# Group ends of a Mamba stage, a second block's first norms, and a first MLP unit, in another order

## What is computed

```python
xBC = jax.nn.silu(causal_depthwise_conv(xBC, conv_w, conv_b))   # 4 taps per channel
...
y = y * lax.rsqrt(jnp.mean(y * y, axis=-1, keepdims=True) + EPS)  # per group of 512
return y.astype(h.dtype) @ w_out
...
return rms_norm(h, g_final)                                     # end of the first block
...
hx = modulate(rms_norm_2(x, norm1), sh1, sc1)                   # start of the second block
ak, av, gk, gv, lrf, lrb, aq, gq, go, ga, gg = jnp.split(hx @ w_in, IN_OFFSETS, axis=-1)
...
x = x + gt2[..., None, :] * sq_relu_mlp(modulate(rms_norm_2(x, norm2), sh2, sc2), w_mlp1, w_mlp2)
```

## Time and profile before

| | |
|---|---|
| median of three runs | 1875.54 us (1874.74 to 1878.44) |
| the profiled execution's own time | 1872.59 us |
| its span, first to last instruction | 1870.8 us |
| TensorE busy in it | 1763.6 us (94%) |
| VectorE, ScalarE, GpSimd busy | 1009.3, 785.4, 716.7 us (54%, 42%, 38%) |
| mean granted TensorE clock | 0.976 of 2.4 GHz |

### The profile page before, as it was taken

How to read it: one execution, slowest core, us unless ns; L and a number is a source line. 1 busy time by engine, 2 the same in 40 slices (tenths; PEclk the granted TensorE clock), 3 DMA queues, 4 the chain that set the end, 5 groups by cost and what they waited for, 6 DMA issues and landing times.

```text
span 1870.8 us, 24943 instructions
## 1 busy us (share of the span) xinstructions
PE 1763.6 (94%) x8893; PEld 1406.8 (75%) x8893; DVE 1009.3 (54%) x1563; ACT 785.4 (42%) x1340; POOL 716.7 (38%) x795
## 2 busy tenths in 40 slices
PE   7998998988999999899999999999999989999998
PEld 5776776766777656678778888888878768888887
DVE  5978685477545784346658837656621442222122
ACT  4444353446446664335552245554432342223231
POOL 3644444532444013321113432223234545555553
PEclk9999999989999999999999999999999989999999
DMA  6332332211223001120108721121123323333332
GB/s 196 91 115 89 112 91 68 68 63 39 68 82 96 12 23 45 49 56 24 35 23 283 235 67 35 35 57 46 46 78 91 89 69 99 93 101 90 101 93 99
DMA packets 238793, 152.04 MB, mean 81 GB/s; under 512 B 7997, under 2 KB 223046, under 8 KB 238694
## 3 DMA queue, kind: packets, MB, share of 16 engines
q1 hardware_dynamic: 225894, 125.54, 23.4%
q10 hardware_dynamic: 12800, 25.17, 4.0%
HBM read 148.59 MB, written 2.10 MB: 81 GB/s over the span
## 4 chain that ended last, share of the span: by engine, by line
PE 75%; DVE 13%; ACT 6%; issue 4%; DMA 1%; SPq 1%; POOL 0%; DVEq 0%; ACTq 0%; POOLq 0%
PE ps L648 19%; PE ps L652 19%; PE ps L649 19%; DVE xs L1295 2%; PE ps L2062 2%; PE ps L2044 1%; PE ps L1545 1%; PE ps L1577 1%; PE ps L2051 1%; PE ps L2505 1%; DMA ada_late<-w_ada 1%; DVE mod_late L2363 1%; DVE queries L1814 1%; PE ps L2045 1%; ACT wh L611 1%
## 5 line engine op out<-in xcount | busy, mean ns | idle before, releaser
L598 POOL TENSOR_TENSOR wl<-raw,wh 128x256 fp32r<-128x256 f32 (+1 forms) x775 | 693.3, 924 | 1091.7 <-ACT wh L611 1091.6
L648 PE MATMUL ps<-ah,wh 128*128 128x512 f32 (+1 forms) x1208 | 492.1, 407 | 18.2 <-DVE al L760 9.2
L652 PE MATMUL ps<-ah,wl 128*128 128x512 f32 (+1 forms) x1208 | 475.2, 393 | 0.1
L649 PE MATMUL ps<-al,wh 128*128 128x512 f32 (+1 forms) x1208 | 475.0, 393 | 0.0
L611 ACT ACTIVATE wh<-raw 128x1024 fp32r<-128x1024 f32 (+1 forms) x220 | 230.8, 1049 | 343.6 <-PE ps L652 329.9
L648 PEld LDWEIGHTS ps<-ah,wh 128*128 128x128 f32 (+1 forms) x1208 | 228.1, 189 | 83.0 <-issue 22.9
L652 PEld LDWEIGHTS ps<-ah,wl 128*128 128x128 f32 (+1 forms) x1208 | 227.9, 189 | 52.7 <-POOL wl L598 1.4
L649 PEld LDWEIGHTS ps<-al,wh 128*128 128x128 f32 (+1 forms) x1208 | 228.6, 189 | 47.4 <-issue 1.7
L648 PE MATMUL ps<-bh,wh 128*128 128x512 f32 (+1 forms) x588 | 236.4, 402 | 19.0 <-DVE resid L1410 13.1
L652 PE MATMUL ps<-bh,wl 128*128 128x512 f32 (+1 forms) x588 | 233.2, 397 | 0.9 <-POOL wl L598 0.8
L649 PE MATMUL ps<-bl,wh 128*128 128x512 f32 (+1 forms) x588 | 232.6, 396 | 0.0
(11 more groups left out here) (409 smaller groups left out, 2575.0 us busy)
## 6 DMA issues: line engine op xcount, KB each, us to landing
raw<-w_mlp SPq DMA_DIRECT2D x64, 512.0 KB, 3.8
raw<-w_in SPq DMA_DIRECT2D x52, 512.0 KB, 3.7
raw<-ssm_w_in SPq DMA_DIRECT2D x40, 512.0 KB, 3.7
ada_late<-w_ada ACTq DMA_DIRECT2D x16, 1024.0 KB, 6.7
ada_raw<-w_ada ACTq DMA_DIRECT2D x16, 512.0 KB, 4.3
raw<-ssm_w_out SPq DMA_DIRECT2D x16, 512.0 KB, 3.4
raw<-mla_w_in SPq DMA_DIRECT2D x11, 512.0 KB, 3.8
raw<-mla_w_out SPq DMA_DIRECT2D x8, 512.0 KB, 3.4
```

The costliest lines, as they stand in the source:

```text
L598: nc.gpsimd.tensor_tensor(wl[:, s, part], raw[:, s, part], wh[:, s, part].bitcast(F32), ALU.subtract).then_inc(lo_ready, LOW_PIECES * (par ...
L648: nc.tensor.matmul(dst, w_hi[k], x_hi[k], start=k == 0, stop=False)
L649: nc.tensor.matmul(dst, w_hi[k], x_lo[k], start=False, stop=False)
L652: ins = nc.tensor.matmul(dst, w_lo[k], x_hi[k], start=False, stop=k == n - 1)
```

## The change

Three places change, and no arithmetic does.

**Group ends.** The newest tap and the bias of each convolution move from VectorE to ScalarE (`newest_tap`, an Identity activation with a scale and a bias per channel) in the three groups that follow the first. Piece 4's is made from PSUM in `take_conv`, piece 5's after the heads, pieces 0 to 3 between the roundings of the norm (`high`). VectorE adds the two halves of the first output unit after its second and its third convolution of x instead of after all. In g = 2 the second output unit moves ahead of `turn_x`.

```diff
@@ -1001,10 +1001,10 @@
                 for n in range(8, 10):
                     projection("ssm", g, n)
                 output("ssm", g, g, 10, 5, 0)
+                output("ssm", g, g, 10, 5, 1)
+                turn_x(g + 1)
                 if g < GROUPS - 2:
-                    output("ssm", g, g, 10, 5, 1)
-                turn_x(g + 1)
-                output("ssm", g, g, 10, 5, 2 if g < GROUPS - 2 else 1)
+                    output("ssm", g, g, 10, 5, 2)
                 turn_b(g + 1)
                 if g < GROUPS - 2:
                     output("ssm", g, g, 10, 5, 3)
@@ -1013,6 +1013,8 @@
             for w in range(4):
                 output("ssm_last", 0, GROUPS - 1, 0, 0, w)
+        conv_column = lambda g, n: g * 4 + n if n < 4 else 16 + 4 * (n - 4) + g
...
@@ -1031,11 +1033,21 @@
         def act_mamba(act):
+            def newest_tap(g, n, src):
+                k = V_CONV + conv_column(g, n)
+                o = xs[:, n] if n < 4 else (bt, ct)[n - 4][:]
+                nc.scalar.activation(o, src, ACT.Identity, scale=V(k + PAD * CCH), bias=V(k + TAPS * CCH))
+            def newest_of(g, n):
+                newest_tap(g, n, conv_in[:, n, PAD:PAD + T])
             def take_conv(stage, i, g, n):
                 if n == 0 and g:
                     act.wait_ge(sem("conv_ready"), g * 6 + AHEAD)
                 act.wait_ge(unit_done, unit(stage, i, n) + 1 + CREDIT)
+                if g and n == 4:
+                    newest_tap(g, n, bank(n % 2))
                 nc.scalar.activation(conv_in[:, n, PAD:PAD + T], bank(n % 2), ACT.Copy).then_inc(acc_free[n % 2], 1)
                 split_ahead(act, stage, i, n)
@@ -1130,6 +1142,9 @@
...
+                act.wait_ge(acc_free[1], g * 9 + ACC0["ssm"][1] + 4)
+                act.wait_ge(sem("mix_ready"), g * GH + GH)
+                newest_of(g + 1, 5)
                 for p in range(4):
                     square(g, p)
                 scale(g)
@@ -1137,7 +1152,12 @@
                 nc.scalar.activation(zs[:, 0], zs[:, 0], ACT.Silu)
                 gate("ssm", g, g + 1, 1)
                 split_ahead(act, "ssm", g, 7)
-                for p in range(4):
+                high(g, 0)
+                for p in range(1, 4):
+                    newest_of(g + 1, p - 1)
+                    if p == 3:
+                        act.wait_ge(sem("gv_ready"), g * 4 + 4)
+                        newest_of(g + 1, 3)
                     high(g, p)
...
@@ -1286,12 +1306,14 @@
             def convolve(stage, i, g, n):
-                tap = lambda k: V(V_CONV + k * CCH + (g * 4 + n if n < 4 else 16 + 4 * (n - 4) + g))
+                tap = lambda k: V(V_CONV + k * CCH + conv_column(g, n))
                 o = xs[:, n] if n < 4 else (bt, ct)[n - 4][:]
                 dve.wait_ge(acc_free[n % 2], i * 9 + (1 + ACC0[stage][n % 2] + n // 2 + 1))
-                st(nc.vector.tensor_scalar(o, conv_in[:, n, PAD:PAD + T], tap(PAD), tap(TAPS), ALU.mult, ALU.add))
+                if g == 0:
+                    st(nc.vector.tensor_scalar(o, conv_in[:, n, PAD:PAD + T], tap(PAD), tap(TAPS), ALU.mult, ALU.add))
                 for k in range(PAD):
-                    st.wait()
+                    if g == 0 or k:
+                        st.wait()
                     ins_ = nc.vector.scalar_tensor_tensor(o, conv_in[:, n, k:k + T], tap(k), o, ALU.mult, ALU.add)
                     if k + 1 < PAD:
                         st(ins_)
...
@@ -1402,9 +1424,9 @@
-            def output(stage, i, n0, w):
+            def output(stage, i, n0, w, halves=(0, 1)):
-                for c in range(2):
+                for c in halves:
@@ -1433,15 +1455,18 @@
                 convolve("ssm", g, g + 1, 4)
                 convolve("ssm", g, g + 1, 5)
                 normed(g)
-                for n in range(4):
-                    convolve("ssm", g, g + 1, n)
+                convolve("ssm", g, g + 1, 0)
+                convolve("ssm", g, g + 1, 1)
+                output("ssm", g, 10, 0, (0,))
+                convolve("ssm", g, g + 1, 2)
+                output("ssm", g, 10, 0, (1,))
+                convolve("ssm", g, g + 1, 3)
                 if g < CTX_BLOCKS // 2:
                     take_modulation(g)
-                output("ssm", g, 10, 0)
+                output("ssm", g, 10, 1)
+                weigh_x(g + 1)
                 if g < GROUPS - 2:
-                    output("ssm", g, 10, 1)
-                weigh_x(g + 1)
-                output("ssm", g, 10, 2 if g < GROUPS - 2 else 1)
+                    output("ssm", g, 10, 2)
                 take_b(g + 1)
                 if g < GROUPS - 2:
                     output("ssm", g, 10, 3)
@@ -1883,12 +1908,12 @@
-        GAINED_BANK = 7
+        GAINED_BANK, FINAL_BANK = 7, 4
         def act_between(act):
             norm_act(act, "norm1", None, D, b=GAINED_BANK, eps=EPS * EPS)
             norm_high(act, "norm1", chunk(ah), lambda j: mod[:, j, 0:1])
-            norm_act(act, "final", None, D, dst=norm_sq[:, 1])
+            norm_act(act, "final", None, D, b=FINAL_BANK, dst=norm_sq[:, 1])
         def dve_between(dve):
@@ -1984,6 +2009,8 @@
                 main, side = K_BANKS[n]
                 if n == 0:
                     pe.wait_ge(acc_free[1], ACC0["gqa"][1] + 1)
+                else:
+                    pe.wait_ge(norm_rstd, 2 * NORM_AT["final"][0] + 1)
                 low = unit_high(pe, "gqa", 0, K_UNIT + n)
                 project(bank(main), "gqa", K_UNIT + n, chunk(ah), chunk(al), DC, P, low=low).then_inc(sem("k_projected"), 1)
                 project_ctx("gqa", K_UNIT + n, bank(side)[:, 0:CTX], P).then_inc(unit_done, 1)
@@ -1995,31 +2022,32 @@
                 nc.tensor.matmul(bank(6), ones[:], k_sq[n][:, 0:T], start=True, stop=True)
                 nc.tensor.matmul(bank(7)[:, 0:CTX], ones[:], k_sq[n][:, T:TA], start=True, stop=True).then_inc(sem("k_sums"), 1)
-            def project_v(half, tiles):
+            lows = {}
+            def project_v(half, tiles, ks=range(V_KS)):
                 s = slot("gqa", half)
-                unit_ready(pe, "gqa", 0, half)
+                if ks[0] == 0:
+                    lows[half] = unit_high(pe, "gqa", 0, half)
                 vh, vl = flat(wh, s, FULL, V_KS), flat(wl, s, FULL, V_KS)
-                for t in tiles:
-                    dst = bank((6, 7, 3)[t // 2])[:, t % 2 * CTX:(t % 2 + 1) * CTX]
-                    hi, lo, tok = (ah, al, t) if t < TT else (ch, cl, t - TT)
-                    tok = slice(tok * P, (tok + 1) * P)
-                    for k in range(V_KS):
-                        c = half * V_KS + k
+                for k in ks:
+                    lows[half](k, KVH * HD)
+                    for t in tiles:
+                        dst = bank((6, 7, 3)[t // 2])[:, t % 2 * CTX:(t % 2 + 1) * CTX]
+                        hi, lo, tok = (ah, al, t) if t < TT else (ch, cl, t - TT)
+                        tok, c = slice(tok * P, (tok + 1) * P), half * V_KS + k
                         nc.tensor.matmul(dst, hi[:, c, tok], vh[:, k], start=half == 0 and k == 0 and t % 2 == 0, stop=False)
                         nc.tensor.matmul(dst, hi[:, c, tok], vl[:, k], start=False, stop=False)
                         ins_ = nc.tensor.matmul(dst, lo[:, c, tok], vh[:, k], start=False, stop=c == DC - 1 and t % 2 == 1)
-                    if half and t in (1, 3):
-                        ins_.then_inc(sem("gv_projected"), 1)
+                        if half and k == V_KS - 1 and t in (1, 3):
+                            ins_.then_inc(sem("gv_projected"), 1)
                 return ins_
-            lows = {}
...
@@ -2064,13 +2092,18 @@
             pe.wait_ge(acc_free[1], ACC0["lr"][1] + 1)
             project_ctx("lr", 0, bank(1, slice(0, 32), slice(0, CTX)), 32).then_inc(sem("lr_ctx"), 1)
+            norm_pe_summed(pe, "norm1", norm_v[:, 2], GAINED_BANK)
+            norm_pe_summed(pe, "final", norm_v[:, 1], FINAL_BANK)
             project_v(0, range(TT, KT))
-            norm_pe_summed(pe, "norm1", norm_v[:, 2], GAINED_BANK)
-            norm_pe_summed(pe, "final", norm_v[:, 1])
             pe.wait_ge(acc_free[0], ACC0["lr"][0] + 1)
-            project(bank(0, slice(0, 32)), "lr", 0, chunk(ah), chunk(al), DC, 32, before=norm_chunk(pe, "norm1")).then_inc(unit_done, 1)
-            pe.wait_ge(norm_rstd, 2 * NORM_AT["final"][0] + 1)
-            project_v(0, range(TT)).then_inc(unit_done, 1)
+            ready = norm_chunk(pe, "norm1")
+            for k in range(DC):
+                lr_done = project(bank(0, slice(0, 32)), "lr", 0, chunk(ah), chunk(al), DC, 32, before=ready, ks=[k])
+                if k == DC - 1:
+                    lr_done.then_inc(unit_done, 1)
+                if k % 2:
+                    v_done = project_v(0, range(TT), [k // 2])
+            v_done.then_inc(unit_done, 1)
             project_v(1, range(KT)).then_inc(unit_done, 1)
             project_q(0, range(DC))
             project_k(0)
```

(23 more changed lines are left out.)

4 lines of the change are left out of this document (2 added, 2 removed).

## The result

The changed kernel takes 1850.53 us (median of four runs, 1849.85 to 1852.46). The kernel before, run beside it, had 1875.14 (four runs, 1867.33 to 1878.44): ratio 0.9876, 95% interval 0.9845 to 0.9908. In a larger set, 19 runs of the kernel before have a median of 1870.26 (1866.27 to 1879.26) and four more of the changed one 1851.91: ratio 0.9893, 0.9865 to 0.9920. So the gain is 18.4 us by the larger set and 24.6 by the smaller, and the kernel before scatters by 13 us from run to run, the changed one by 3.

What follows compares the result with a forecast made beforehand. TensorE, busy 94% of the span, was taken as the bound, with waits and half clock to save: 8.4 + 7.4 + 5.5 + 5.8 + 1.3 = 28.4 us off 1872.6 gives 1844.2, plus 2.9 is 1847; range 1841 to 1856, some 83%.

Steps and rivals of the forecast that it cites:

- First two group ends: Norm's end to transposes in g = 0 and 1: removing TensorE's waits and half clock gains 8.4 and 7.4 us.
- ScalarE's later split: First output unit's split arrives some 0.6 us later; in g = 0 and 1 TensorE does modulation sums first, no loss.
- Third group end: Group end g = 2, first output unit to the heads: 18.3 us becomes 12.2, gain 5.5 after 0.6 for late split.
- the new wait before the state: Group end g = 2: no unit lies between transposes and state any more, so some 0.9 us of waiting stays open.
- Second block: Start of the second block: earlier sums and alternating lr and value matmuls gain 5.8 us, bounds 3.5 and 6.8.
- the wait before value unit 1: Second block: ScalarE may split for unit 1 only after lr is done, so TensorE waits 1.0 us.
- MLP: First MLP units: alternation gains 1.3 us, bounds 0 and 2, with half clock taken for 4.8 us at the start.
- Rival (c): Low clock comes elsewhere, as later gaps move: up to 4 us either way, 1843 to 1852; 71% together with the forecast.
- Rival (a): Second block and MLP: stretches alternate as written but at 1.2 GHz throughout; gain 10.4 us, time 1865; 4%.
- (b): Group ends: VectorE late at the transposes by 2.3 us or less, clock falls; 3 to 11 us back, middle 1853; 19%.
- (d): Group ends: ScalarE becomes the bound, splitting the first output unit late; whole turns negative at 9.5 us each, 1879; 2%.
- (e): Stalls only change places: as (b), and value and MLP splits return the second block's gains; under 4 us left, 1873; 4%.

Runs made afterwards that it cites:

- Experiment 8: Changed kernel with the modulation's one-column matmuls of the first two groups spread between the chunks of the two following projections: median 1849.27 us, ratio to before 0.9886.
- `both`: Changed kernel with spread modulation matmuls, and the first output unit's gate and split moved ahead in all three groups: 1843.71 us, ratio to before 0.9862.

## Why the prediction was nearly right

The forecast was 1847 us with 1841 to 1856, the result 1850.5: inside, on the slow side. Part of that is luck. The forecast's start, 2.9 us above the profiled execution, was the median of three executions, 1875.54; 19 runs of the same kernel have 1870.26. From there the same terms give 1842, and the gain of 28.5 us stands against 18.4 measured with the larger set and 24.6 with the smaller. Point by point:

**First two group ends,** 8.4 and 7.4 forecast, 7.4 and 5.9 measured. By the clock of the two traces VectorE's chain seems to match: first half added at 175.74 (forecast 175.7), second at 179.30 (179.4), last silu done 182.20 (182.4), transposes 183.03 (183.0). That is luck: the norm's sum stands at 155.15 before and 154.18 after. Counted from it, the steps come 1.0, 0.9 and 0.8 us later than forecast, and the transposes 28.85 us behind it instead of 27.85. The order of the steps was right. VectorE's rows for the two halves, and ScalarE's for the silu:

```profile
175.05 0.69 DVE L1432 TENSOR_TENSOR resid<-resid,ps 128x512 f32<-128x512 f32 x1 [1.19 <-PE ps L652]
...
178.62 0.68 DVE L1432 TENSOR_TENSOR resid<-resid,ps 128x512 f32<-128x512 f32 x1
```

```profile
181.57 0.63 ACT L1083 ACTIVATE xs<-xs 128x512 f32<-128x512 f32 x1 [2.20 <-DVE xs L1317]
```

The step that failed is the one that took ScalarE's later split as hidden by the modulation sums ("TensorE first has the modulation sums to do and does not notice"), a cost of nothing in the sum. Experiment 8 and `both` show what stands in its place: without any low clock the transposes still come at 28.84 and 28.85 us, 1.0 and 0.9 later than the sum had them, and with the split moved ahead as well at 26.94 and 26.96. The low clock behind the sums, which the first trace of before did not show in group 0, was missed too: in group 0 its 3.4 us cost nothing beside this chain, in group 1 its 6.8 us cost 0.6.

**Third group end,** 5.5 forecast, 6.0 measured in a trace without a low stretch there, 5.3 in the trace of the group ends alone, with one; against the other three traces of the old code, 5.0. The late split cost 0.7 us (forecast 0.6), the new wait before the state 0.63 (0.9).

**Second block,** 5.8 forecast, 5.5 measured, split 3.4 and 2.1 where the text had 3.5 and 2.3; the wait before value unit 1 is 1.09 (forecast 1.0).

**MLP,** 1.3 forecast, 0.3 to 0.9 at equal low clock: mis-sized. The wait before unit 2 is 0.28 us in the trace (0.5 to 1 forecast). The low stretch ended 2.8 us behind the start there, where 4.8 was forecast.

**Rival (c) was sized too small:** "up to 4 us either way", with a middle of zero. Outside the changed places the stages lost 4.5 us in this pair of traces, the larger part of the 5.7 that the profiled execution lies above the forecast's 1844.2. Between the two traces of the kernel before, the rest of the second block moved by +3.1 us, the rest of the first by +2.3 and the heads by -1.1. Rival (a), half clock throughout, is refuted: the second block's stage has no low clock in any of the nine traces with the alternation, and the MLP's runs at full clock once the low stretch that stood there already is over (19 matmuls in 4 us):

```profile
1490.00:1494.00 4.00, 4.00 (x19) 3.26 (x18) 4.00 (x7) 2.17 (x3) 0.00 (x0) 1.00 0.01 4
```

The Trainium skill, page "TensorE: Matmul & The Clock Gate", section "A second HAM failure mode: psum-queue depth-cycling", tells of another kernel whose clock swung while it cycled through PSUM banks; in this trace no swing follows from the alternation. (b) did not come: the silus end 0.8 to 0.9 us ahead of the transposes in all three groups. (d) was closer than its 2%: ScalarE did become a bound of the group ends, and its sign, TensorE waiting for `wh` at an output unit, stands in the third group with 2.50 us (1.85 before); but it is far from the 9.5 us a group that would have turned the gain. The sign of being right that failed is the clock of 1.00 at the first two group ends. (e) is refuted by the stage table.

**Left open:** what decides which gaps bring the low clock in an execution, and whether the changed kernel's smaller scatter (3 us in 8 runs against 13) comes from having fewer gaps. The group ends alone scatter by 8 us in four runs.

## What to carry to other kernels

Judge a change of a few us by the length of the changed stage between two fixed instructions, read at equal low-clock time, and not by the kernel's total: here a real gain of 5.5 us was invisible in the median of ten runs, and a step worth 2.1 us looked like a loss. Where only totals are at hand, set each run's time beside its own granted clock first: that took the scatter here from 13 us to a deviation of 0.9. When a stall on one engine goes, look for a distance that stays the same to 0.02 us in every group and every variant: it names the chain that bounds next, even where no wait is shown. Moving work to a second engine pays only if nothing that the first one waits for stands behind it there.

## What was not expected of the hardware

The clock can fall without any wait of TensorE. Behind 32 one-column matmuls (row at 155.04 above, 3.63 us busy throughout) the window 158 to 162 had 0.58 in the changed kernel and 262 to 266 had 0.50. Over all traces, such a low stretch begins within the block or at most 0.9 us behind it at 20 of 22 blocks in eleven traces, and at none of the six places in three traces where the same matmuls stand in bursts of four between others. Whether the single column or something else about the block does it isn't separated here. In both windows of the changed kernel TensorE is busy for the whole 4 us, and the third row is the kernel with the bursts:

```profile
158.00:162.00 4.00, 4.00 (x15) 3.22 (x16) 2.09 (x4) 3.99 (x6) 0.77 (x2) 0.58 0.01 2
...
262.00:266.00 4.00, 4.00 (x14) 3.42 (x15) 2.08 (x4) 3.99 (x7) 1.11 (x2) 0.50 0.00 0
```

```profile
155.00:159.00 4.00, 4.00 (x26) 3.48 (x25) 2.73 (x4) 3.96 (x6) 0.00 (x0) 1.00 0.01 2
```
